# The final RMSNorm of a two-layer streaming encoder, done by column chunks during the last output block

## The reference

```python
def _rmsnorm(x, g):
    xf = x.astype(jnp.float32)
    y = xf * lax.rsqrt(jnp.mean(xf * xf, axis=-1, keepdims=True) + EPS) * g.astype(jnp.float32)
    return y.astype(x.dtype)
...
    y = hs.astype(x.dtype) * jax.nn.silu(gate)
    return x + y @ w_out, new_conv, hs[:, -1]      # w_out: 1536 x 1024
...
# after both layers: y_prompt = _rmsnorm(xp, norm_final), y_sample = _rmsnorm(xs, norm_final)
```

## Time and profile before

| what | us |
|---|---|
| median of 3 runs | 1565.19 (1564.01 to 1571.38) |
| the profiled execution, its own time | 1566.23 |
| its span in the profile | 1564.4 |
| TensorE busy (matmuls) | 1489.1, 95% of the span |
| VectorE busy | 837.5, 54% |
| GpSimd busy | 682.5, 44% |
| ScalarE busy | 451.1, 29% |

### The profile page before, as it was taken

How to read it: one execution, slowest core, us unless ns; L and a number is a source line. 1 busy time by engine, 2 the same in 40 slices (tenths; PEclk the granted TensorE clock), 3 DMA queues, 4 the chain that set the end, 5 groups by cost and what they waited for, 6 DMA issues and landing times.

```text
span 1564.4 us, 23445 instructions
## 1 busy us (share of the span) xinstructions
PE 1489.1 (95%) x9332; PEld 1416.4 (91%) x9332; DVE 837.5 (54%) x1181; ACT 451.1 (29%) x766; POOL 682.5 (44%) x461
## 2 busy tenths in 40 slices
PE   6999999999999999999999999889999999989994
PEld 5999888887789999899989999789999999989993
DVE  7112556557555347353393110688878878792114
ACT  5111434445532221221150001235153351460000
POOL 5353222222124334243345444357566665656550
PEclk9999999999999999999999999999999999999996
DMA  4311010100010011100113322111111111122222
GB/s 185 107 61 37 32 44 28 44 28 28 19 37 27 32 47 44 35 27 31 48 46 121 98 78 87 42 41 55 43 52 54 41 54 50 46 71 96 86 79 115
DMA packets 27416, 89.77 MB, mean 57 GB/s; under 512 B 3600, under 2 KB 6736, under 8 KB 27344
## 3 DMA queue, kind: packets, MB, share of 16 engines
q1 hardware_dynamic: 16560, 60.34, 11.0%
q10 hardware_dynamic: 10784, 28.39, 5.5%
HBM read 77.16 MB, written 11.68 MB: 57 GB/s over the span
## 4 chain that ended last, share of the span: by engine, by line
PE 79%; DVE 10%; issue 5%; POOL 3%; ACT 2%; DMA 0%; ACTq 0%; POOLq 0%; DVEq 0%; SPq 0%
PE ps L358 48%; PE ps L525 11%; PE ps L401 7%; PE ps L464 2%; PE ps L498 2%; PE ps L485 2%; POOL w_hi L329 1%; DVE Y L1482 1%; DVE H L1058 1%; POOL w_lo L333 1%; PE ps L601 1%; PE ps L585 1%; PE ps L596 1%; DVE arena L1500 1%; DVE arena L1544 1%
## 5 line engine op out<-in xcount | busy, mean ns | idle before, releaser
L329 POOL TENSOR_TENSOR w_hi<-raw,ones 128x512 fp32r<-128x512 f32 x228 | 332.7, 1459 | 828.5 <-PE ps L358 507.4
L358 PE MATMUL ps<-H,w_hi 128*128 128x364 f32 x2832 | 578.0, 331 | 32.0 <-DVE H L1058 20.9
L358 PEld LDWEIGHTS ps<-H,w_hi 128*128 128x128 f32 x2832 | 485.0, 189 | 38.5 <-issue 22.6
L358 PE MATMUL ps<-H,w_lo 128*128 128x364 f32 x1752 | 387.8, 330 | 0.0
L333 POOL TENSOR_TENSOR w_lo<-raw,w_hi 128x512 fp32r<-128x512 f32 x228 | 351.1, 1540 | 17.9
L358 PEld LDWEIGHTS ps<-H,w_lo 128*128 128x128 f32 x1752 | 306.7, 189 | 0.0
L358 PE MATMUL ps<-Yr,w_hi 128*128 128x364 f32 x672 | 149.1, 330 | 0.0
L525 PE MATMUL ps<-H,w_hi 128*128 128x364 f32 x672 | 144.1, 338 | 0.8 <-DVE Y L1177 0.8
L401 PE MATMUL ps<-w_hi,H 128*128 128x256 f32 (+1 forms) x720 | 132.4, 284 | 2.9 <-ACT Y L781 1.2
L1404 DVE TENSOR_TENSOR arena<-ps,arena 128x1092 f32 (+1 forms) x16 | 20.7, 1295 | 206.7 <-PE ps L358 206.7
L525 PEld LDWEIGHTS ps<-H,w_hi 128*128 128x128 f32 x672 | 111.7, 188 | 14.8 <-issue 10.9
(11 more groups left out here) (174 smaller groups left out, 1682.5 us busy)
## 6 DMA issues: line engine op xcount, KB each, us to landing
raw<-weights SPq DMA_DIRECT2D x114, 512.0 KB, 3.5
arena<-xT ACTq DMA_DIRECT2D x15, 546.0 KB, 4.7
x_scratch<-arena ACTq DMA_DIRECT2D x8, 546.0 KB, 5.5
arena<-x_scratch ACTq DMA_DIRECT2D x8, 546.0 KB, 3.6
yT<-arena ACTq DMA_DIRECT2D x8, 546.0 KB, 2.9
arena<-k_scratch ACTq DMA_DIRECT2D x8, 304.0 KB, 4.7
k_scratch<-Y ACTq DMA_DIRECT2D x2, 512.0 KB, 2.7
arena<-xT SPq DMA_DIRECT2D x1, 546.0 KB, 5.0
```

The source lines that it names most:

```text
L329: pool.tensor_tensor(w_hi[:, s, cols].rearrange("p (k n) -> p k n", n=P), raw[:, s, cols].rearrange("p (k n) -> p k n", n=P), every_tile_ones,
L358: mm = pe.matmul(sets[st][:, c, 0:CW], lw[:, s, w], rx[:, k, c * CW:(c + 1) * CW], start=(first and n == 0 and m == 0), stop=(last and n = ...
```

## The change

Layer 1's last pair is taken apart. Pairs 0 to 2 run as before. Then block 6 runs alone over its two pieces, and block 7 after it in three column chunks, `TAIL` = (0, 512), (512, 896), (896, 1088), each over all twelve weight tiles, in banks 3, 4 and 5. The padding piece at the end of the weights is dropped, and SP loads the last pieces in the new order.

For each chunk there is a separate add, square, accumulate, sums over partitions, mean, root, reciprocal, diagonal and broadcast. TensorE's program has the sums of chunk 0 before row 5 of chunk 1 and its broadcast before row 10; the sums of chunk 1 before row 7 of chunk 2; broadcast 1, sums 2 and broadcast 2 after the last matmul. Chunk 2's factors are broadcast twice, into banks 0 and 2. VectorE scales blocks 3 to 7 of each chunk from PSUM. ScalarE multiplies blocks 0 to 2 by the gain beforehand, behind the squares of blocks 4 to 6, and copies the factors of a chunk to `rb` in SBUF; GpSimd multiplies blocks 0 to 2 by them. SP, not ScalarE, issues the output: three writes per chunk, for blocks 0 to 2, 3 to 5, and 6 and 7. The core of the diff, VectorE's, TensorE's and SP's parts:

```diff
+TAIL = ((0, 512), (512, 896), (896, LIVE))
+TAIL_BANK = (6, 7, 0)
+POOL_ROWS = 3
...
+            for c, (a, b) in enumerate(TAIL):
+                mid = POOL_ROWS + rows // 2 + 1
+                for k0, k1, ready, count in ((0, POOL_ROWS, xp_done, POOL_ROWS * (c + 1)),
+                                             (POOL_ROWS, mid, xn_done, rows * c + mid - POOL_ROWS),
+                                             (mid, KD, xn_done, rows * (c + 1))):
+                    sp.wait_ge(ready, count)
+                    sp.dma_start(yT[k0:k1, :, a:b].rearrange("k p n -> p k n"), X[:, k0:k1, a:b]).then_inc(y_saved, 16)
...
+            for c, (a, b) in enumerate(TAIL):
+                for k in range(POOL_ROWS):
+                    pool.wait_ge(xg_done, k + 1)
+                    pool.wait_ge(rb7_done, c + 1)
+                    pool.tensor_tensor(X[:, k, a:b], X[:, k, a:b], rb[:, a:b], ALU.mult).then_inc(xp_done, 1)
...
+                for c, (a, b) in enumerate(TAIL):
+                    for row in range(KC):
+                        if (c, row) == (1, 5):
+                            tail_sums(0)
+                        if (c, row) == (1, 10):
+                            tail_broadcast(0)
+                        if (c, row) == (2, 7):
+                            tail_sums(1)
...
+                        for m, (lw, rx) in enumerate(((w_hi, H), (w_lo, H), (w_hi, Yr))):
+                            mm = pe.matmul(ps[:, 3 + c, 0:b - a], lw[:, piece % 2, k * P:(k + 1) * P], rx[:, row, a:b],
+                                           start=(row == 0 and m == 0), stop=(row == KC - 1 and m == 2))
+                    mm.then_inc(tail_done, 1)
+                tail_broadcast(1)
+                tail_sums(2)
+                tail_broadcast(2)
...
+                    if not even and b >= KD - 1 - POOL_ROWS:
+                        k = b - (KD - 1 - POOL_ROWS)
+                        act.activation(X[:, k, :], X[:, k, :], ACT.Copy,
+                                       scale=vecs[:, VC_N[2] + k:VC_N[2] + k + 1]).then_inc(xg_done, 1)
...
-            norm_roots(2)
-            for b in range(KD):
-                act.wait_ge(xn_done, b + 1)
-                act.dma_start(yT[b], X[:, b, :]).then_inc(y_saved, 16)
-            act.wait_ge(y_saved, 16 * KD)
...
+            tail_square(0)
+            tail_roots(0)
+            tail_copy(0)
+            tail_square(1)
+            tail_roots(1)
+            tail_square(2)
+            tail_copy(1)
+            tail_roots(2)
+            tail_copy(2)
...
-            norm_factors(2)
-            dve.wait_ge(bc_done, 3)
-            for b in range(KD):
-                g = vecs[:, VC_N[2] + b:VC_N[2] + b + 1]
-                for x, r in ((X[:, b, 0:SEQ], ps[:, 6:8, :].rearrange("p a n -> p (a n)")),
-                             (X[:, b, SEQ:TOK], ps[:, 2, CW:CW + TOK - SEQ])):
-                    done = dve.scalar_tensor_tensor(x, x, g, r, ALU.mult, ALU.mult)
-                done.then_inc(xn_done, 1)
...
+            def tail_scale(c, rows):
+                a, b = TAIL[c]
+                dve.wait_ge(bc7_done, c + 1)
+                if c < 2:
+                    dve.wait_ge(rb7_done, c + 1)
+                for k in rows:
+                    g = vecs[:, VC_N[2] + k:VC_N[2] + k + 1]
+                    dve.scalar_tensor_tensor(X[:, k, a:b], X[:, k, a:b], g, ps[:, TAIL_BANK[c], 0:b - a],
+                                             ALU.mult, ALU.mult).then_inc(xn_done, 1)
+
+            tail_add(0)
+            tail_acc(0)
+            tail_mean(0)
+            tail_inverse(0)
+            tail_scale(0, range(3, 6))
+            tail_add(1)
+            tail_scale(0, range(6, 7))
+            tail_acc(1)
+            tail_scale(0, range(7, 8))
+            tail_mean(1)
+            tail_inverse(1)
+            tail_add(2)
+            tail_acc(2)
+            tail_scale(1, range(3, 5))
+            tail_mean(2)
+            tail_inverse(2)
+            tail_scale(1, range(5, 8))
+            tail_scale(2, range(3, 8))
```

More of the change, by code:

```diff
@@ L95, with tail_tiles @@
 ARENA = 14400
+TAIL = ((0, 512), (512, 896), (896, LIVE))
+TAIL_BANK = (6, 7, 0)
+POOL_ROWS = 3
+def tail_tiles(c):
+    a, b = TAIL[c]
+    return range(a // P, -(-b // P))
 def one(t, k):
@@ L308, in load, with load_run, queries_first, by_block @@
                 sp.dma_start(raw[:, s, :], one(weights, piece)).then_inc(w_in[s], 16)
[L310 to L318, removed]
+            def load_run(first, last, order=None):
+                if order is not None:
+                    for n in range(first, last):
+                        load(n // 2, n % 2, order(n))
+                    return
+                with sp.Fori(first // 2, last // 2) as i:
+                    for s in range(2):
+                        load(i, s, 2 * i + s)
+            def queries_first(n):
+                a, b = divmod(n - PC_A, A_PCS)
+                return PC_A + A_PCS * a + (b + 2) % A_PCS if 1 <= a < A_KV else n
+            def by_block(end):
+                return lambda n: {end - 3: end - 2, end - 2: end - 3}.get(n, n)
+            load_run(2, PC_B0 + 1, queries_first)
+            load_run(PC_B0 + 1, PIECES - 5)
+            load_run(PIECES - 5, PIECES, by_block(PIECES))
+            rows = KD - POOL_ROWS
+            for c, (a, b) in enumerate(TAIL):
[5 more added lines that the diff above has]
+                    sp.dma_start(yT[k0:k1, :, a:b].rearrange("k p n -> p k n"), X[:, k0:k1, a:b]).then_inc(y_saved, 16)
+            sp.wait_ge(y_saved, 16 * 9)
         @block.gpsimd
@@ L705, in _, with last_blocks @@
                     odd_group(i, p)
-            out_projection(6, PC_OO, USE_OO, MIX)
-            sum_squares(2)
-            broadcast(2, 2)
+            def last_blocks():
+                base = PIECES - 4
+                pe.wait_ge(drained[0], USE_OO[0] + KD // 2 - 1)
+                for n in range(2):
+                    piece = base + n
+                    project(piece % 2, range(6 * n, 6 * n + 6), piece, H, Yr, 0, first=n == 0, last=n == 1)\
+                        .then_inc(piece_done, 1)
+                pe.wait_ge(drained[1], USE_OO[1] + KD // 2 - 1)
+                for c, (a, b) in enumerate(TAIL):
[6 more added lines that the diff above has]
+                            tail_sums(1)
+                        half, k = divmod(row, 6)
+                        piece = base + 2 + half
+                        if c == 0 and k % 4 == 0:
+                            pe.wait_ge(w_split, 2 * piece + (k // 4 + 1))
+                        for m, (lw, rx) in enumerate(((w_hi, H), (w_lo, H), (w_hi, Yr))):
[5 more added lines that the diff above has]
+                tail_broadcast(2)
@@ new lines, in tail_sums, with tail_broadcast @@
+            def tail_sums(c):
+                pe.wait_ge(acc7_done, c + 1)
+                if c == 0:
+                    pe.wait_ge(drained[0], USE_OO[0] + KD // 2)
+                for t in tail_tiles(c):
+                    m = tile_rows(t)
+                    mm = pe.matmul(ps[0:m, 1, t:t + 1], acc[:, t * P:t * P + m], ones[:, 0:1], start=True, stop=True)
+                mm.then_inc(ssq7_done, 1)
+            def tail_broadcast(c):
+                pe.wait_ge(diag7_done, c + 1)
+                tiles = tail_tiles(c)
+                a, b = TAIL[c]
+                for bank in ((TAIL_BANK[c],), (TAIL_BANK[c],), (TAIL_BANK[c], 2))[c]:
+                    pe.matmul(ps[:, bank, 0:b - a], ones,
+                              diag[:, tiles[0]:tiles[-1] + 1, :].rearrange("p t n -> p (t n)")[:, 0:b - a],
+                              start=True, stop=True).then_inc(bc7_done, 1)
@@ L711, in _ @@
+            out_projection(6, PC_OO, USE_OO, MIX, 1)
+            last_blocks()
         @block.scalar
@@ L956, in out_residual @@
                     act.dma_start(res[:, s, :], src[s]).then_inc(res_in[s], 16)
-                for b in range(KD):
+                for b in range(KD if even else KD - 1):
                     i, s = b // 2, b % 2
@@ new lines, in tail_acc, with tail_mean @@
+            def tail_acc(c):
+                a, b = TAIL[c]
+                dve.wait_ge(sq7_done, c + 1)
+                dve.wait_ge(acc_done, 3 * KD - 1)
+                dve.tensor_tensor(acc[:, a:b], acc[:, a:b], sq[:, a:b], ALU.add).then_inc(acc7_done, 1)
+            def tail_mean(c):
+                tiles = tail_tiles(c)
+                dve.wait_ge(ssq7_done, c + 1)
+                parts = [(P, tiles[0], tiles[-1] + 1)] if c < 2 else [(P, tiles[0], tiles[-1]), (DEC, NT - 1, NT)]
+                for r, t0, t1 in parts:
+                    mm = dve.tensor_scalar(rT[0:r, t0:t1], ps[0:r, 1, t0:t1], 1.0 / DM, EPS, ALU.mult, ALU.add)
+                mm.then_inc(ms7_done, 1)
```

62 lines of the change are left out of this document (52 added, 10 removed).

## The result

| | before | after |
|---|---|---|
| median, us | 1570.8 (20 runs, 1564.01 to 1575.63) | 1558.01 (20 runs, 1553.09 to 1568.89) |
| profiled execution, us | 1566.23 | 1558.85 |
| its span, us | 1564.4 | 1556.7 |
| block 7's first matmul at | 1517.5 | 1519.3 |
| tail, from there to the end of the span | 46.9 | 37.4 |

The ratio to the kernel before is 0.9938, 95% interval 0.9923 to 0.9952: 9.7 us less (7.5 to 12.1). I had forecast 13.9 us less and 1551.3, with a range up to 1556.5, which the median of 1558.0 leaves.

The account below looks back on a forecast made before the run. TensorE carries 79% of the chain; the change works on the 28.7 us relay behind the last projection matmul. Span 1564.4 to 1550.5 is 13.9 us less, giving 1551.3 on the median's scale; range 1549.3 to 1556.5.

Parts of the forecast that it names:

- The relay: After the last projection matmul, add, norm, broadcast, scaling and output run one after another without overlap: a 28.7 us tail.
- one table load: ScalarE's table load for the root, 1.28 us, falls into idle gaps: zero cost, at most 1.3 once.
- The added wait: TensorE stands 1.3 us before the sums of columns 512 to 895, as VectorE's scalings precede its second add.
- the accumulate at 0.56: VectorE's accumulate for columns 512 to 895, summed in the schedule at 0.56 us.
- rival B: VectorE and GpSimd get in each other's way; scalings stretched by 1.8 would give 1557; chance 0.09.
- rival A: TensorE's clock falls inside the tail, during its 1.3 us wait: 2.2 us on the path, 1553.5; chance 0.22.
- Chunks one and two are written under all this: Output of columns 0 to 895 is written beside the remaining tail work, so only the last three writes count.
- the last three writes: Final output writes from SP: 0.80 us each to issue, 2.3 to land, issued from 1546.3, landing at 1550.2.
- my sum: Tail schedule across engines: GpSimd's last rows end at 1546.3, then the last writes; span 1550.5.
- C: Output costs by the row, 10.8 ns whatever its length: writes take 33 us, 1570.7, slower; chance 0.04.
- DMA engines full behind 1547: Sign in the trace that would show output writes costing by the row instead of by the byte.
- D: In-order engines wait more, the first scaling starts only with the last chunk, tail stays a relay: 1558; chance 0.07.

Follow-up runs that it names:

- The order alone: Kernel before with only the last pieces reordered (block 6 alone, then block 7 in three ranges of 364 columns), old norm and output: ratio 0.9999, tail 46.8 us.
- the half rows: Changed kernel with the three writes of columns 512 to 895 each cut into two of 192 columns: tail 38.2 us, 0.8 more.

## Why the prediction was wrong, point by point

**The relay and what cuts it: right.** Nothing waits up to the first scaling; it began 16.25 into the tail, 16.1 by the schedule. Chunk matmuls of 512 and 384 columns were 0.231 and 0.174 us apart, those of 192 0.111 (20 starts, 1535.66 to 1537.88, ahead of the wait); 0.231, 0.175 and 0.109 were forecast. Scalings took 740, 610 and 410 ns, as forecast. The order alone gave nothing, and the tail's one table load, 1.28 us, lay beside block 7's first chunks.

**The added wait: right in kind, short in size.** I put 1.3 us before the second sums; it was 1.6. The step that failed is the accumulate at 0.56: it took 1.07 beside GpSimd, and 0.56 without GpSimd. That is rival B on an operation with two SBUF inputs, while the scalings with one PSUM operand never stretched. The Trainium skill, "GPSIMD Engine Reference", Specifications, says that GpSimd contends with VectorE instructions that have two SBUF inputs. The trace agrees with it. I had named the accumulates as the ones to stretch, and then summed them at the undisturbed price. Cost 0.5 us.

**The clock: rival A happened.** It fell 22.5 to 22.8 into the tail in four of the five profiles with the changed kernel's engine order, and at 26.5 in the fifth. With TensorE kept busy the tail is 1.0 shorter. I gave it 0.22 and 2.2 us; it was the likely case at half the price. What I weighed wrongly: I compared its wait with the 4 us pause of before and overlooked that the clock fell there at 1540, when matmuls had just begun again, so a fall doesn't need a pause that lasts up to it. The Trainium skill, "TensorE: Matmul & The Clock Gate", Part 1, has the full clock depend on recent work, and the trace agrees in that each fall came behind a stretch of waiting and short work.

**The output: the step that failed most.** "Chunks one and two are written under all this" was false for the second of them (columns 512 to 895). SP waits first for GpSimd's three rows of it. By my own schedule these were ready at 1544.2 (copy at 1541.3, three rows of 0.98). In the kernel before, the first byte moved 0.8 us behind its issue, and the span ended 0.9 behind the last byte. With these and 2.36 MB at the 403 GB/s of the earlier trace rows, 5.9 us, the estimate is 1551.8, 1.3 us above the 1550.5 that I wrote, with no error in the engines' schedule at all. I had priced the last three writes by issue and landing and not by what was in the queue ahead of them. SP's waits in program order made it worse: 3 us without a byte, then 2.36 MB at once. Writing by readiness gave 2.2 back.

**The sum.** The tail was 4.6 us longer than forecast (37.4 against 32.8). The end followed chunk one's GpSimd rows and the bytes behind them, not GpSimd's last row on which my sum stood: that row was 3.0 late (31.6 against 28.6), and writing by readiness took 2.2 off the end without moving it. Along the path that counted, chunk one's rows were ready at 28.5 in place of 26.5. Of these 2.0 about 1.0 is the clock, 0.5 the accumulate, and the rest small things that no run separates. Behind them came 8.9 us of writes, in place of the 6.3 that my schedule of engines and last issues left: 2.6 for bytes in the queue that I had put at nothing. The single edits don't add up to this, since they hide each other.

**The base.** The forecast was a difference put on the median of three runs. On the base of the 20 runs, 1570.8, a difference of 13.9 us would have given 1556.9, above my range too; on the other medians of the kernel before, 1566.4 to 1567.3, it would have given 1552.5 to 1553.4, within it. The measured difference of 9.7 would have given 1556.7 to 1557.6 on these medians, just outside, and 1555.5 on my own base, within. So the 4 us that I missed put the time at the edge of the range, and the draw of the runs, which is luck, put it clearly outside. My range had no room for three runs being quick ones, though they alone spread over 7 us.

**Other rivals.** C is measured and small. The sign that I had named for it, DMA engines full behind 1547, did appear (1549 to 1555), but from the bytes: it doesn't tell a price by the row from a full queue, and only the half rows did. D didn't happen: chunk zero's scaling began as the last of chunk one's matmuls ran, not with the last chunk. The gain is faster by 0.6% on the middle value, just over the half per cent that I put 0.87 on; its interval, 0.48 to 0.77%, includes that line.

## What to carry to other kernels

When work is moved under other work, schedule the output too: bytes by the measured rate, from the moment at which they are ready, in the order in which the issuing queue waits for them; a chain of engines doesn't show it, the DMA share in the windows does. In an in-order engine put first what another engine waits for (one add ahead of three scalings came with 2.5 us less here, of which about 1 goes with the clock), and write each piece when it is ready. Compare short edits at the end of a kernel by the stretch that they touch, since 10 us of spread ahead of it hide them in the totals.

## What the runs showed of the hardware

- VectorE's accumulate with two SBUF inputs of 384 columns took 0.56 us without GpSimd, 1.07 with GpSimd beside it for part, 1.49 with GpSimd beside it all the time. Scalings with one PSUM operand took 737 to 742 ns at 512 columns in all three cases.
- Five profiles in which TensorE, VectorE, ScalarE and GpSimd run the same program saw TensorE's clock fall at 22.5, 22.5, 22.6, 22.8 and 26.5 us into the tail. A fall is not a fixed point of the program. In the changed kernel the longest idle stretch of TensorE in block 7 ahead of the fall was 1.6 us, and matmuls were running when it came.
- Writes from SBUF went at 361 to 403 GB/s with rows of 1536 to 4368 bytes and at 309 to 335 with 768 bytes, the DMA engines full in both cases.
- 192-column matmuls, each with its own weight load, came 0.111 us apart. Those of 256 columns come every 0.118 and those of one column every 0.109: narrowing a chunk from 256 to 192 columns saved 0.007 us a matmul.
